# Block one's mixing stage as one weave of four paced streams, with rope tables, the fetch of x and the last product rearranged

## The reference, cut to what matters

```
h = rms_norm(x, norm_mix_pre[l]);  proj = h @ w_in[l]
(c_q, c_kv, k_rope, sc_b, sc_c, sc_x, cf_a, cf_g, gm_u, gm_v, gate_logits) = split(proj)
y_a = mla_branch(c_q, c_kv, k_rope, cos, sin, ...) @ w_o_mla[l]       # attention, 8 heads
y_b = (sc_b * conv3(sc_c * sc_x)) @ w_o_sc[l]                         # short convolution
y_c = silu(layer_norm(conv31(cf_a * sigmoid(cf_g)))) @ w_o_cf[l]      # 31 taps for each channel
y_d = (gelu(gm_u) * (ws @ layer_norm(gelu(gm_v)) + bs)) @ w_o_gm[l]
g = sigmoid(gate_logits + gate_b[l])                                  # 4 x 1024 gates
merged = g[0]*y_a + g[1]*y_b + g[2]*y_c + g[3]*y_d
x = x + rms_norm(merged @ w_out[l], norm_mix_post[l])
```

## Time and profile before

| what | value |
|---|---|
| median of 3 runs | 3140.14 us (3139.28 to 3142.92) |
| the profiled execution, its own time | 3139.51 us |
| its span, first to last instruction | 3137.7 us |
| TensorE busy | 2814.8 us (90%) |
| VectorE busy | 2058.8 us (66%) |
| ScalarE busy | 1279.8 us (41%) |
| third merge product of layer 0 starts, counted from the span's start | 339.38 us |

### The profile page before, as it was taken

One profiled execution on the slowest core, in us unless ns is written; L12 is line 12 of the kernel. 1 busy time (PEld: TensorE's weight loads), 2 busy tenths in 40 slices (PEclk: granted clock), 3 DMA queues, 4 the chain that ended last, 5 costly groups with the idle time before them and its releaser, 6 DMA issues.

```text
span 3137.7 us, 59458 instructions
## 1 busy us (share of the span) xinstructions
PE 2814.8 (90%) x24380; PEld 2710.2 (86%) x24380; DVE 2058.8 (66%) x3649; ACT 1279.8 (41%) x1981; POOL 4.4 (0%) x10
## 2 busy tenths in 40 slices
PE   6879889989788899789788998898787999999999
PEld 6768889988778899778788998787777999999999
DVE  5778657557776674776456767674656666666665
ACT  3434344434434444333244443333343444444443
POOL 0000000000000000000000000000000000000000
PEclk9889899989898999889799999899898999999999
DMA  5433335535334454322142553212233555555554
GB/s 176 148 128 118 128 131 188 183 119 170 117 105 150 144 187 139 116 68 69 55 144 99 189 189 124 77 66 68 96 107 117 173 185 191 173 178 193 185 183 159
DMA packets 143053, 434.16 MB, mean 138 GB/s; under 512 B 15777, under 2 KB 26273, under 8 KB 142529
## 3 DMA queue, kind: packets, MB, share of 16 engines
q1 hardware_dynamic: 138112, 423.63, 41.1%
q10 hardware_dynamic: 4672, 6.72, 0.7%
HBM read 429.25 MB, written 1.05 MB: 137 GB/s over the span
## 4 chain that ended last, share of the span: by engine, by line
PE 72%; DVE 17%; ACT 5%; issue 4%; DMA 1%; DVEq 0%; ACTq 0%; SPq 0%
PE ps L1525 21%; PE ps L1527 20%; PE ps L1526 20%; PE ps L1530 10%; DVE wl L2218 4%; DVE b L2222 3%; DVE b L2230 3%; DVE SC L2230 2%; ACT wh L1919 2%; DVE SC L2222 1%; DVE RS L2222 1%; ACT b L1929 1%; PE ps L1533 1%; ACT SC L1998 1%; DVE RS L2227 0%
## 5 line engine op out<-in xcount | busy, mean ns | idle before, releaser
L2218 DVE TENSOR_TENSOR wl<-wf,wh 128x1024 fp32r<-128x1024 f32 (+2 forms) x850 | 960.2, 1164 | 324.8 <-ACT wh L1919 323.1
L1525 PE MATMUL ps<-b,wh 128*128 128x256 f32 x3712 | 1073.7, 289 | 97.7 <-DVE wl L2218 40.6
L1527 PE MATMUL ps<-b,wl 128*128 128x256 f32 x3712 | 1060.3, 286 | 0.0
L1526 PE MATMUL ps<-b,wh 128*128 128x256 f32 x3712 | 1059.5, 285 | 0.0
L1919 ACT ACTIVATE wh<-wf 128x1024 fp32r<-128x1024 f32 (+2 forms) x850 | 822.6, 1004 | 357.8 <-PE ps L1527 292.6
L1525 PEld LDWEIGHTS ps<-b,wh 128*128 128x128 f32 x3712 | 723.3, 195 | 111.7 <-issue 83.2
L1525 PE MATMUL ps<-HH,wh 128*128 128x256 f32 x2496 | 732.4, 293 | 56.9 <-DVE wl L2218 52.4
L1526 PEld LDWEIGHTS ps<-b,wh 128*128 128x128 f32 x3712 | 723.3, 195 | 0.2
L1526 PE MATMUL ps<-HL,wh 128*128 128x256 f32 x2496 | 721.5, 289 | 0.0
L1527 PEld LDWEIGHTS ps<-b,wl 128*128 128x128 f32 x3712 | 721.2, 194 | 0.0
L1527 PE MATMUL ps<-HH,wl 128*128 128x256 f32 x2496 | 720.5, 289 | 0.0
(11 more groups left out here) (189 smaller groups left out, 1837.8 us busy)
## 6 DMA issues: line engine op xcount, KB each, us to landing
wf<-in_w_in_b SPq DMA_DIRECT2D x112, 512.0 KB, 4.1
wf<-in_moe_wg SPq DMA_DIRECT2D x88, 512.0 KB, 3.3
wf<-in_moe_wu SPq DMA_DIRECT2D x88, 512.0 KB, 4.3
wf<-in_w_in SPq DMA_DIRECT2D x80, 512.0 KB, 4.1
wf<-in_moe_wd SPq DMA_DIRECT2D x64, 384.0 KB, 3.2
wf<-in_w_ffn_g SPq DMA_DIRECT2D x44, 512.0 KB, 3.3
wf<-in_w_ffn_u SPq DMA_DIRECT2D x44, 512.0 KB, 4.3
wf<-in_moe_wd SPq DMA_DIRECT2D x64, 320.0 KB, 3.5
```

Source lines behind the costliest of these rows:

```text
L1525: e.matmul(o, stat[0], mov[0], start=first, stop=False)
L1526: e.matmul(o, stat[0], mov[1], start=False, stop=False)
L1527: return e.matmul(o, stat[1], mov[0], start=False, stop=end)
L2218: e.tensor_tensor(u.wlo, u.buf, u.whi.bitcast(F32), SUB).then_inc(u.lo[0])
```

## The change

- **One weave.** The weave of `products1` and `norms` is gone. The latent norms (now both at once, `together`), the rotary key, queries and attention are one stream `main`, each part with its own pace; the two `glu` products stand at the head of `gating`; `conv` waits for them. The order of the streams is gating, main, rest, conv.
- **Rope tables.** Block one's tables are made at the program's very start, cos ahead of the parts of x, sin ahead of units 2 and 3; block two's, in a tile of their own (ROPE2), during the last product of block one's second feed-forward stage (`y_out`, 6 units for each of 4 steps), cos after its second step, sin after its third.
- **x first.** x is fetched on SP's queue ahead of units 0 and 1, the constants after these.
- **Late row blocks last.** `gemm_late`: of `y_out` in block one's and `add_x` in block two's mixing stages, the first two steps (4 units) are made over k = 0 to 5 first, then over k = 6, 7.
- **Norm of the long convolution.** `conv_silu` becomes `conv_z` for both halves and then `conv_y` for both, with one DVE instruction less for each half; the factor 0.5 moves into the split.

```diff
@@ tables of weights
-    WT0 = [1.0, 0.55]
-    WT1, IW1, GW = [0.77, 0.96, 0.72, 1.58], [1.17, 1.18], 7
+    WT0 = [1.7, 0.67]
+    WT1, GW, W1N, W1K, W1Q, W1A, W1R = [9.69, 0.65, 1.0, 5.0], 5, 6.0, 5.75, 5.63, 7.77, 6.0
@@ def start
         if stage_no[0] == 0:
+            tables = rope_tables(ins["positions"], VEC[:, NVEC - 2:NVEC - 1], (COS, SIN))
+            next(tables)
             for p in range(4):
                 xp = x_parts(p)
                 x_squares(p)
                 x_low(xp)
+                if p == 1:
+                    step("first_units").split_to = AHEAD
+            rope[0] = finish(tables)
@@
+    def gemm_late(kind, banks, rhs, rdy, fields):
+
+        w = Wide(kind, banks[:2], rhs, rdy)
+        w.part(0, 6)
+        yield
+        w.part(6, 8)
+        w.take_out(fields, None)
+        yield
+        yield from gemm(kind, banks[2:], 8, rhs, rdy, lambda n, st: fields(n + 2, st), True)
@@ def block1_mix
-        weave([products1(), norms()], IW1)
@@ def conv
+            while len(az) < 2:
+                yield
@@ def main
+            yield from paced(together(latent_norm("q", 0, "qn"), latent_norm("k", 2, "kvn")), W1N)
+            yield from paced(rope_key(), W1K)
+            cq, ck = latent["q"], latent["k"]
+            yield from paced(queries(cq, ck), W1Q)
+            od = yield from paced(attention(8, ...), W1A)
@@ def gating
+            yield from gemm("glu", pairs(wb, 16, 4), 8, rhs, hall, to_g)
...
-        weave([main(), rest(), conv(), gating()], WT1)
+        weave([gating(), main(), rest(), conv()], WT1)
...
-        yield from gemm("y_out", pairs(ins["w_out"][l], 0, 8), 8, kcols(M2), {k: mt[k // 2] for k in range(8)}, y_out(Y, "npo", l, gread, ys, yd), True)
+        yield from gemm_late("y_out", pairs(ins["w_out"][l], 0, 8), kcols(M2), {k: mt[k // 2] for k in range(8)}, y_out(Y, "npo", l, gread, ys, yd))
@@ def block1_ffn
+        tables = rope_tables(ins["positions_2"], VEC[:, NVEC - 1:NVEC], (COS2, SIN2))
+        for n, _ in enumerate(gemm("y_out", ..., 22, kcols(F2), fd, y_out(Y, "nfo", l, None, ys, yd), True)):
+            if l and n == 1:
+                next(tables)
+            if l and n == 2:
+                rope[1] = finish(tables)
+            yield
@@ def conv_z on DVE (before: conv_silu)
+            for t in (2 * p, 2 * p + 1):
+                ins = stt(CY[:, t, :], CY[:, t, :], vec("clg", st.l, t), st.bk.ps[:, 0:S], MUL, MUL)
...
+            for t in (2 * p, 2 * p + 1):
+                ins = ts(CY[:, t, :], CY[:, t, :], vec("clb", st.l, t), None, ADD)
@@ def sp_program
         e.dma_start(VEC[:, :], ins["vecs"]).then_inc(t_vec[0], 16)
-        e.dma_start(CST[:, :], ins["cst"]).then_inc(t_cst[0], 16)
+        for i in range(4):
+            e.dma_start(X[:, i * 512:(i + 1) * 512], ins["xT"][:, i * 512:(i + 1) * 512]).then_inc(t_x[i][0], 16)
         for u in units:
+            if u.i == 2:
+                e.dma_start(CST[:, :], ins["cst"]).then_inc(t_cst[0], 16)
```

More of the change, by code:

```diff
@@ L120, in paced, with together @@
 def paced(g, cost):
-    for _ in g:
-        yield cost
+    while True:
+        try:
+            next(g)
+        except StopIteration as e:
+            return e.value
+        yield cost
+def together(*gens):
+    gens = list(gens)
+    while gens:
+        for g in list(gens):
+            try:
+                next(g)
+            except StopIteration:
+                gens.remove(g)
+        yield
 def drive(g):
@@ L684, in block1_mix, with latent_norm, rope_key @@
         latent, kr_done = {}, []
-        def norms():
-            if rope[0] is None:
-                rope[0] = rope_tables(ins["positions"], IF1)
-            latent["q"] = (yield from rmsnorm(C[:, 0:2, :], 2, "qn", l, [x[:, 0:2, :] for x in CP2], cd))[0]
-            yield
-            latent["k"] = (yield from rmsnorm(C[:, 2:4, :], 2, "kvn", l, [x[:, 2:4, :] for x in CP2], cd))[0]
-            yield
+        def latent_norm(key, b0, gain):
+            c2 = [x[:, b0:b0 + 2, :] for x in CP2]
+            latent[key] = (yield from rmsnorm(C[:, b0:b0 + 2, :], 2, gain, l, c2, [cd[b0 // 2]]))[0]
+        def rope_key():
             sc = Scr.take()
@@ L713, in to_g @@
             az.append(st.done)
-        def products1():
-            yield from gemm("glu", pairs(wb, 16, 4), 8, rhs, hall, to_g)
-        weave([products1(), norms()], IW1)
-        cq, ck = latent["q"], latent["k"]
         late = {}
         def conv():
+            while len(az) < 2:
+                yield
             for k in range(31):
@@ L744, in conv @@
                 st.z, st.th = P.next("conv_z"), P.next("conv_th")
-                st.done = st.sc.out = P.next("conv_y")
-                out2.append(split([x[:, 2 * p:2 * p + 2, :] for x in CYS], CY[:, 2 * p:2 * p + 2, :], st.done))
+                zs.append(st)
                 yield
-            late["y"] = out2
+            for z in zs:
+                st = step("conv_y")
+                st.a = z
+                st.done = z.sc.out = P.next("conv_y")
+                z.done = st.done
+                yield
+            late["y"] = [split([x[:, 2 * p:2 * p + 2, :] for x in CYS], CY[:, 2 * p:2 * p + 2, :], z.done, 0.5) for p, z in enumerate(zs)]
+            yield
         def gelu_fields(st, w, dst, src):
@@ L823, in to_u @@
                 ud.append(st.done)
-            yield from gemm("gelu", pairs(wb, 20, 4), 8, rhs, hall, to_u)
+            yield from paced(gemm("gelu", pairs(wb, 20, 4), 8, rhs, hall, to_u), W1R)
             st = step("values2")
@@ L2884, in sp_program @@
             E.wait_ge(t_out[i])
-    HAS_UNITS = {"wide", "copy_rs", "up_gate", "shift_rs", "y_out", "copy", "glu", "times", "gelu", "gate1", "gate2", "merge", "up", "add_x", "add_x0", "shift", "q", "values1", "values2",
+    HAS_UNITS = {"first_units", "wide", "copy_rs", "up_gate", "shift_rs", "y_out", "copy", "glu", "times", "gelu", "gate1", "gate2", "merge", "up", "add_x", "add_x0", "shift", "q", "values1", "values2",
                  "values3", "keys2"}
```

188 lines of the change are left out of this document (101 added, 87 removed).

## The result

| | us |
|---|---|
| before, median of 4 runs | 3139.7 (3138.8 to 3142.9) |
| changed, median of 4 runs | 3059.0 (3055.1 to 3065.0) |
| ratio | 0.9743, 95% interval 0.9724 to 0.9761 |
| forecast | 3077.5 (3056 to 3110) |

The account below looks back on a forecast made before the run. Mixing stages were taken as bound by DVE in some stretches, latency in others, PE in few, with order deciding. Terms -35.7 - 28.8 - 4.6 + 3 - 3.4 - 3.4 gave -73, cut to -62: 3077.5 us (3056 to 3110).

Parts of the forecast that it names:

- Latents and rotary key: Mixing stage, first `glu` product to first gate product: 40.4 us with PE as the bound, chains standing beside full products.
- To the end of `values2`: Mixing stage, first gate product to the row-layout product's end: 50 us, with PE waiting about 4 behind the short convolution.
- Row norms to the first gate product with attention: Mixing stage after `values2`: 44.6 us of DVE work plus 2.4 for low clock, 47 us until DVE's pair.
- Attention, 86.4 us: Mixing stage's attention stretch: led by DVE, same work as before within 1 us, so again 86.4 us.
- Tail, 23 us: Mixing stage, from the last gate product: 23 us with the z, z, y, y order, against 26.58 before.
- The 5.5 us off for each layer: Both mixing stages: 5.5 us less gain per layer than the walk, since an old stretch outran its count; total -73 became -62.
- Start, +3: Program start: first product near 13.8, units 2 and 3 near 22.4; +3 us, bounds -2 and +6.
- Tables of block two: Block two's start gains 8.6 and 1.5 us; feed-forward loses 4.7 of wait and 2 at low clock; net -3.4.
- Late row blocks: Last products of the mixing stages: four waits of 3.25 us shrink; -1.2 each in block one, -0.5 in block two.
- Half of it is given back in DVE's queue: Rival: ACT and DVE wait for each other in the two middle stretches, 15 us more per layer; 3108 us, chance 0.22.
- Slower: the low clock takes hold: Rival: low clock in middle stretches and a third of attention costs 60 us a layer; 3198 us, chance 0.03.
- The idle is only moved by a third: Rival: DVE's and ACT's queues run as walked without slip and the tail closes; 3060 us, chance 0.06 for below 3060.

Follow-up runs that it names:

- e6: Changed kernel with every second tap of the long convolution from the 11th on left out on DVE; 3057.5 us, ratio 0.9737 to the kernel before.
- e5: Changed kernel with the two weaves and mixing-stage order of the kernel before, all else as changed; 3121.7 us, ratio 0.9945 to the kernel before.
- e8: Changed kernel with block two's tables put back at the start of block two; 3063.4 us, ratio 0.9755 to the kernel before.
- e1: Changed kernel with late row blocks kept in block one alone, block two's add_x as before; 3049.6 us, ratio 0.9715 to the kernel before.
- e11: Changed kernel with late row blocks in block one alone, block one's tables behind the first products' first half, block two's tables in three pieces; 3038.1 us, ratio 0.9676.
- e3: Changed kernel with block one's tables made behind the first half of the first two products, x's parts ahead; 3052.4 us, ratio 0.9721.
- e7: Changed kernel with the short convolution cut to one of its three taps; 3051.3 us, ratio 0.9714 to the kernel before.

## Why the prediction was right in direction and low in size

- **What bounds the kernel.** Right: the two mixing stages gain 74.4 us, and the low clock behind them another 5.5. The other parts together lose 5.4 us, as block two alone lost 13.4.
- **Latents and rotary key, 40.4 us.** Measured 40.60. The step held whole: thirteen units one after the other with the chains beside them.
- **To the end of `values2`, 50 us.** Measured 53.11, DVE busy for 45.54 where I counted 45.5. The wait behind the short convolution, "about 4", was 4.33; the one of 2.06 in `values2` and the clock of 0.90 I had not in the sum.
- **Row norms to the first gate product with attention.** "47 us until DVE's pair for the next gate product": mis-sized. That product starts 39.52 us after `values2`, and DVE's pair for it starts at 191.65, after 36.9 us. Four things in my sum don't belong there: one head's softmax (2.8), which stands behind that pair; one of the four taps (1.7) and one of the ten low parts (1.2), as the stretch has three and nine; and 2.4 us for the low clock, which PE had (0.87) but which, as I read it, did not stretch DVE's list. The remaining 2 us I can't place. The wait behind the second norm was forecast at about 8 and was 6.80; the 3.35 behind the first was not forecast.
- **Attention, 86.4 us.** Measured 84.09 from product to product. The size is close for the wrong reason: e6 shows that PE leads there, not DVE.
- **Tail, 23 us.** Measured 23.44. The third merge product starts at 301.78, where I put "near 300".
- **The 5.5 us off for each layer.** This step failed. I took them off since the stretch 98.20:189.32 was longer than its count. The counts of the new stretches came out at 245 against 240.8 and 239.3: over the whole stage no slip, but 4 to 6 us too many. A slip of 3 us did come in the first two stretches (93.7 for 90.4), and the row norms took back more. e5 takes 268 us with the same work in the old order, so most of what a stage of before had above its count was its order, and that is what the change removes. A surplus measured on the old order was charged to the new one. That it was so in the one stretch that I took it from is argued and not shown.
- **Behind the mixing stages.** Not in the forecast: the low clock behind the wait of 6.37 went with it, 2.7 us in each layer.
- **Start, +3.** Measured +4.6 with the wait of 2.29 that went, inside the bounds. First product at 14.55 (13.8 forecast), units 2 and 3 at 22.87 (22.4).
- **Tables of block two.** +6.1 (forecast +6.7) and -10.9 (-10.1); the wait in the third `y_out` step 3.34 for 4.7. e8 confirms both ends.
- **Late row blocks.** Block one -1.4 and -1.8 for -1.2 each. Block two, "-0.5", has the wrong sign: +3.7 and +2.7. I saw that both banks end together and delay x's parts, and did not follow it to the squares and the sums behind them. "3.25 down to about 2 in four places" held in block one (1.84) and not in block two, where 3.56 and 3.55 stand behind the 1.84.

The rivals. "Half of it is given back in DVE's queue" did not come: in the whole stage low parts waited 1.5 us for ACT, against 22.5 before, as the row of DVE's groups from 61.0 to 301.8 says (busy, mean ns, idle before):

```profile
L2283 DVE TENSOR_TENSOR wl<-wf,wh 128x1024 fp32r<-128x1024 f32 x64 | 75.6, 1219 | 1.9 <-ACT wh L1986 1.5
```

"Slower: the low clock takes hold" did not come either: the clock was 0.90 and 0.87 in the two middle stretches, 1.00 in attention. The rule of the Trainium skill (TensorE: Matmul & The Clock Gate, "HAM oscillation — how this bites in real kernels") that I weighed would have stretched the 47 us by 15. The trace has 39.52 there, so it did not decide.

"The idle is only moved by a third" (3060), with DVE's and ACT's queues running without slip and the tail closing, is the one that came nearest, in its number and in what it says of the queues. I gave 0.06 to everything below 3060, and 0.66 to the 3060 to 3095 of the forecast: the median, 3059.0, lies just below these.

The forecast of 3077.5 is 18 us above the median. By the traces: 21 us too little in the mixing stages (11 of it the slip), 6 us too little behind them (5.5 of it the clock), and 15 us given back elsewhere that I had not forecast, nearly all in block two. The other 6 us are the profiled execution, which took 3065.0 where the median is 3059.0.

Of the 13.4 us that block two lost, the late row blocks are 6.4 by their own stretches. The rest is no single place: PE has the same 15670 instructions there and is busy for 8.7 us longer, DVE for no longer, which is the low clock in more places. The same code took 1819.4 to 1827.5 us in that part in the nine runs that keep it, and 1811.2 to 1817.3 in the four without late row blocks there. So that part has a scatter of up to 8 us between runs, and the changed kernel's traced execution lies at its upper end.

That the median fell inside the stated range, 3 us above its lower end, is in part luck: errors of 27 us one way and 15 us the other. Without what block two gave back it would have lain below the range.

## What to carry to other kernels

Read a wait in the view of waits together with the busy time of the engine that ends it, over the whole stretch. Where that engine is busy for nearly 90% of the stretch, moving its work moved the wait (4.33 became 0.98 + 2.14 + more later, in two moves tried), and less work shortened the stretch; where it is busy for less and waits itself, order is worth a lot (28 us in each layer here). Look in the trace whether an edit of a weight moved what it was meant to move. An engine's time from one mark to the next is no count of its work: take some of the work away and see whether the stretch gets shorter. And when two units of work are made to end together, follow the next two engines behind them, not only the one that you relieve.

## What the runs showed of the hardware

The same instructions, in the same place of the program, can run at either level of the clock in kernels that differ elsewhere. In block two, layer 0, nothing in the code of this part differs between the changed kernel and e1, but a stretch of small products and four units took 43.92 us in the one and 38.32 in the other; the kernel before has the slow version too:

```profile
1417.31:1461.23 43.92, 34.54 (x237) 30.71 (x237) 18.31 (x39) 10.27 (x19) 0.00 (x0) 0.69 0.20 73
...
1418.76 0.90 PE L1600 MATMUL ps<-CST,SC 128*128 128x128 f32 x3
```

```profile
1417.17:1455.49 38.32, 28.33 (x236) 25.44 (x236) 18.30 (x39) 10.24 (x19) 0.00 (x0) 0.87 0.24 83
...
1417.97 0.55 PE L1600 MATMUL ps<-CST,SC 128*128 128x128 f32 x3
```

```profile
1506.03:1549.95 43.92, 34.55 (x237) 30.72 (x237) 18.30 (x39) 10.27 (x19) 0.00 (x0) 0.69 0.22 73
```

The granted clock is 0.87 in e1 and 0.69 in the two others; the same three matrix instructions take 0.90 us at the low level (1.2 GHz) and 0.55 at the high one. In both traces the products just ahead, up to 1416, run at the high level; then PE waits 0.93, 0.70 and 0.64 us for ACT between bursts of small products, and behind the first of these waits the two part. All fourteen traces have this stretch: 38.3 us in e1, e6 and e11, 40.1 to 41.3 in six, 43.9 in the kernel before, the changed kernel, e3, e7 and e8, at clocks from 0.87 down to 0.69 and with 18.3 us of DVE work in each. e1 and e3 ran on the same chip, and so did e6 and e7, so it isn't the chip. Which it gets seems to hang on little: the places of the changed kernel's and e1's differ by 0.14 us against the start. What tips it I did not test.

The Trainium skill (TensorE: Matmul & The Clock Gate, "HAM oscillation — how this bites in real kernels") describes products that fall back to the low level again and again because each burst is shorter than the wait behind it. This trace is another case: its first waits, 0.64 to 0.93 us, are shorter than the bursts between them (2.35 us for the first in the changed kernel, 1.34 in e1), and the level still fell in one kernel and not in the other, at a price of 5.6 us. Only one execution of each kernel was traced, so whether this also makes the changed kernel's four executions scatter by 10 us isn't shown. It is a reason why single spans (e1 is 14.5 us under the changed kernel by span, 9.4 by median) have to be read with their stretches.
